# A hybrid decoder layer in float32 on one core: the activations of the weight products stored as even tokens, then odd ones, and read from the two halves in turn

## What is computed

```python
x = x + 0.5 * swiglu(rmsnorm(x), ffn1_w_gate, ffn1_w_up, ffn1_w_down)   # 2048 -> 5504 -> 2048
h = rmsnorm(x)
z = h @ w_in                                    # 2048 -> 3*1536 (q, k, v) + 1024 (u) + 2*2048 (gates)
att = dilated window attention of q, k, v in three groups of 4 heads     # 512 wide
s_out = glu(gelu(s5_ssm(u)))                                             # 1024 wide, with glu_w
merged = sigmoid(gate_a) * (att @ w_attn_branch) + sigmoid(gate_s) * (s_out @ w_ssm_branch)
x = x + merged @ w_out
x = x + 0.5 * swiglu(rmsnorm(x), ffn2_w_gate, ffn2_w_up, ffn2_w_down)
```

## Time and profile before

| | |
|---|---|
| median of 3 runs | 2240.59 us |
| span of the profiled execution | 2237.8 us |
| TensorE matmul, weight load busy | 2230.9 us, 2215.1 us |
| VectorE, ScalarE, GpSimd busy | 1347.1, 1014.1, 479.8 us |
| granted TensorE clock | 1.00 throughout |
| DMA | 528.53 MB, mean 236 GB/s |

### The profile page before, as it was taken

The page is one execution under the profiler, slowest core; times in us unless marked ns, Lnnn a source line. Parts: engine busy times, 40 slices in busy tenths (PEclk is TensorE's granted clock), DMA queues, the critical chain, the costliest instruction groups (busy, mean ns, idle before and its releaser), DMA issues.

```text
span 2237.8 us, 48675 instructions
## 1 busy us (share of the span) xinstructions
PE 2230.9 (100%) x19150; PEld 2215.1 (99%) x19150; DVE 1347.1 (60%) x1422; ACT 1014.1 (45%) x1295; POOL 479.8 (21%) x530
## 2 busy tenths in 40 slices
PE   9999999999999999999999999999999999999999
PEld 9999999999999999999999999999999999999999
DVE  7556557665455756766658867665554555545555
ACT  6554344343334545554455665444433344433443
POOL 2684313420000205664306630100000000000000
PEclk9999999999999999999999999999999999999999
DMA  7976788877776788759868875577877778777764
GB/s 239 275 236 207 241 244 273 263 236 244 244 237 206 227 262 261 218 183 317 273 193 286 260 235 188 178 230 242 260 230 229 240 242 261 227 228 241 242 202 148
DMA packets 441052, 528.53 MB, mean 236 GB/s; under 512 B 41376, under 2 KB 421712, under 8 KB 437104
## 3 DMA queue, kind: packets, MB, share of 16 engines
q1 hardware_dynamic: 425760, 508.64, 72.2%
q0 software_dynamic: 3248, 11.62, 1.5%
q10 hardware_dynamic: 11936, 6.77, 1.0%
HBM read 507.80 MB, written 106.09 MB: 274 GB/s over the span
## 4 chain that ended last, share of the span: by engine, by line
PE 99%; DMA 0%; DVE 0%; ACT 0%; SPq 0%; POOL 0%; issue 0%; POOLq 0%; ACTq 0%
PE pa L1460 32%; PE pa L1462 32%; PE pa L1461 32%; PE pb L1742 0%; DMA raw<-in_ffn_w_gate 0%; PE pb L1647 0%; PE pb L1748 0%; PE pb L1781 0%; PE pb L1707 0%; PE pb L1685 0%; PE pb L1665 0%; PE pb L1770 0%; PE pb L1581 0%; PE pb L1692 0%; PE pb L1566 0%; PE pb L1530 0%
## 5 line engine op out<-in xcount | busy, mean ns | idle before, releaser
L1015 DVE TENSOR_TENSOR w_lo<-raw,w_hi 128x1024 fp32r<-128x1024 f32 x735 | 934.9, 1282 | 620.0 <-ACT w_hi L618 615.4
L1460 PE MATMUL pa<-xg_hi,w_hi 128*128 128x264 f32 x3960 | 1131.4, 286 | 1.2 <-DVE w_lo L1015 1.2
L1461 PE MATMUL pa<-xg_lo,w_hi 128*128 128x264 f32 x3960 | 1125.2, 284 | 0.0
L1462 PE MATMUL pa<-xg_hi,w_lo 128*128 128x264 f32 x3960 | 1123.8, 284 | 0.0
L618 ACT ACTIVATE w_hi<-raw 128x1024 fp32r<-128x1024 f32 x735 | 769.1, 1056 | 754.8 <-PE pa L1462 717.0
L1460 PEld LDWEIGHTS pa<-xg_hi,w_hi 128*128 128x128 f32 x3960 | 745.3, 188 | 8.4 <-issue 6.5
L1462 PEld LDWEIGHTS pa<-xg_hi,w_lo 128*128 128x128 f32 x3960 | 744.2, 188 | 0.0
L1461 PEld LDWEIGHTS pa<-xg_lo,w_hi 128*128 128x128 f32 x3960 | 743.9, 188 | 0.2
L1461 PE MATMUL pa<-act_lo,w_hi 128*128 128x264 f32 x1632 | 463.9, 284 | 0.0
L1460 PE MATMUL pa<-act_hi,w_hi 128*128 128x264 f32 x1632 | 463.5, 284 | 0.0
L1462 PE MATMUL pa<-act_hi,w_lo 128*128 128x264 f32 x1632 | 463.1, 284 | 0.0
(11 more groups left out here) (346 smaller groups left out, 1490.2 us busy)
## 6 DMA issues: line engine op xcount, KB each, us to landing
raw<-in_ffn_w_up SPq DMA_DIRECT2D x172, 512.0 KB, 5.1
raw<-in_ffn_w_gate SPq DMA_DIRECT2D x171, 512.0 KB, 4.8
out_kv_s<-in_cache_kv_w SPq DMA_DIRECT2D x165, 512.0 KB
raw<-in_ffn_w_down SPq DMA_DIRECT2D x160, 512.0 KB, 4.5
raw<-in_w_in SPq DMA_DIRECT2D x152, 512.0 KB, 4.8
raw<-in_w_out SPq DMA_DIRECT2D x32, 512.0 KB, 4.4
tab<-ssm_tab SPq DMA_DIRECT2D x8, 1152.0 KB, 9.4
raw<-in_w_ssm_branch SPq DMA_DIRECT2D x16, 512.0 KB, 4.5
```

What stands on the lines that cost most here:

```text
L1015: dve.tensor_tensor(w_lo[:, slot], raw[:, slot], w_hi[:, slot].bitcast(f32), ALU.subtract).then_inc(lo_ready, 1)
L1460: pe.matmul(out, wh, hi, start=first, stop=False)
L1461: pe.matmul(out, wh, lo, start=False, stop=False)
L1462: return pe.matmul(out, wl, hi, start=False, stop=last)
```

## The change

Every hi and lo operand keeps its place and size, but within a tile of 264 columns the 132 even tokens stand first and the 132 odd ones behind them (halves). The splits read their source with a step of two and write the two halves (by_parity on the source). The matmuls read the operand with a pattern of two dimensions, 132 steps of one element outside and 2 steps of 132 elements inside (in_order), so that the columns enter in the order of the tokens and PSUM, its readers and all else stay as they were. For the first slab and the attention output, where prompt and sample columns are written apart, H0 and H1 name their parts of a half. No instruction is added or removed.

```diff
+    def halves(ap):
+        return ap.rearrange("p n (i j) -> p n i j", i=2)
+    def by_parity(ap):
+        return ap.rearrange("p n (j i) -> p n i j", i=2)
+    def in_order(ap):
+        return ap.rearrange("p (i j) -> p j i", i=2)
+    H0, H1 = slice(0, NT // 2), slice(NT // 2, T // 2)
...
-                    ins = act.activation(xg_hi[:, bass.ds(2 * c + u, 1), :], x_t[:, bass.ds(2 * c + u, 1), :],
+                    ins = act.activation(halves(xg_hi[:, bass.ds(2 * c + u, 1), :]), by_parity(x_t[:, bass.ds(2 * c + u, 1), :]),
                                          ACT.Copy, scale=vec[:, bass.ds(gain0 + 2 * c + u, 1)])
...
-                    ins = act.activation(xg_hi[:, k, 0:NT], pb[:, c % 4, u * NT:(u + 1) * NT], ACT.Copy, scale=vec[:, k:k + 1])
+                    ins = act.activation(in_order(xg_hi[:, k, :])[:, H0], pb[:, c % 4, u * NT:(u + 1) * NT].rearrange("p (j i) -> p j i", i=2),
+                                         ACT.Copy, scale=vec[:, k:k + 1])
...
-                                act.activation(act_hi[:, bass.ds(tile0, w), :], hid_v[:, 0:w], ACT.Copy).then_inc(acthi_ready, 1)
+                                act.activation(halves(act_hi[:, bass.ds(tile0, w), :]), by_parity(hid_v[:, 0:w]), ACT.Copy).then_inc(acthi_ready, 1)
...
-                    ins = dve.scalar_tensor_tensor(xg_lo[:, bass.ds(k, 1), :], x_t[:, bass.ds(k, 1), :],
-                                                   vec[:, bass.ds(gain0 + k, 1)], xg_hi[:, bass.ds(k, 1), :].bitcast(f32),
+                    ins = dve.scalar_tensor_tensor(halves(xg_lo[:, bass.ds(k, 1), :]), by_parity(x_t[:, bass.ds(k, 1), :]),
+                                                   vec[:, bass.ds(gain0 + k, 1)], halves(xg_hi[:, bass.ds(k, 1), :].bitcast(f32)),
                                                    ALU.mult, ALU.subtract)
...
-                                dve.tensor_tensor(act_lo[:, bass.ds(tile0, w), :], hid_v[:, 0:w],
-                                                  act_hi[:, bass.ds(tile0, w), :].bitcast(f32), ALU.subtract).then_inc(actlo_ready, 1)
+                                dve.tensor_tensor(halves(act_lo[:, bass.ds(tile0, w), :]), by_parity(hid_v[:, 0:w]),
+                                                  halves(act_hi[:, bass.ds(tile0, w), :].bitcast(f32)), ALU.subtract).then_inc(actlo_ready, 1)
...
-                pe.matmul(out, wh, hi, start=first, stop=False)
-                pe.matmul(out, wh, lo, start=False, stop=False)
-                return pe.matmul(out, wl, hi, start=False, stop=last)
+                pe.matmul(out, wh, in_order(hi), start=first, stop=False)
+                pe.matmul(out, wh, in_order(lo), start=False, stop=False)
+                return pe.matmul(out, wl, in_order(hi), start=False, stop=last)
```

More of the change, by code:

```diff
@@ L648, in sample_hi @@
                 act.wait_ge(xs_ready, 1)
-                act.activation(xg_hi[:, :, NT:T], xs_g[:], ACT.Copy).then_inc(xs_hi, 1)
+                act.activation(halves(xg_hi[:])[:, :, :, H1], by_parity(xs_g[:]), ACT.Copy).then_inc(xs_hi, 1)
             def first_split_hi(half, ready):
@@ L815, in attention @@
                     act.wait_ge(prod_ready, len(UNITS))
-                    act.activation(att_hi[:, 0:3, 0:NT], att_v[:, 0:3, 0:NT], ACT.Copy).then_inc(att_hi_ready, 1)
+                    act.activation(halves(att_hi[:, 0:3])[:, :, :, H0], by_parity(att_v[:, 0:3, 0:NT]), ACT.Copy).then_inc(att_hi_ready, 1)
                 if i == 5 and j == 0:
@@ L863, in gates_b @@
                         act.wait_ge(att_read, NSLOT)
-                        act.activation(att_hi[:, 3, 0:NT], att_v[:, 3, 0:NT], ACT.Copy).then_inc(att_hi_ready, 1)
+                        act.activation(halves(att_hi[:, 3:4])[:, :, :, H0], by_parity(att_v[:, 3:4, 0:NT]), ACT.Copy).then_inc(att_hi_ready, 1)
                     if isinstance(i, int) and i == ph.iters - 1 and j == 6:
                         act.wait_ge(pv_read, NS)
-                        act.activation(att_hi[:, :, NT:T], att_v[:, :, NT:T], ACT.Copy).then_inc(att_hi_ready, 1)
+                        act.activation(halves(att_hi[:])[:, :, :, H1], by_parity(att_v[:, :, NT:T]), ACT.Copy).then_inc(att_hi_ready, 1)
             def sigmoid(c):
@@ L953, in _ @@
                         act.wait_ge(gelu_ready, 2 * n + 2)
-                        act.activation(zs_hi[:, half], zs_v[:, half], ACT.Copy).then_inc(zhi_ready, 1)
+                        act.activation(halves(zs_hi[:, half]), by_parity(zs_v[:, half]), ACT.Copy).then_inc(zhi_ready, 1)
             def glu(i, ph=PH["glu"]):
@@ L968, in glu @@
                         act.wait_ge(evacuated, ph.group(i, g) + 1)
-                        act.activation(s_hi[:, 2 * c:2 * c + 2], up_v[:], ACT.Copy).then_inc(shi_ready, 1)
+                        act.activation(halves(s_hi[:, 2 * c:2 * c + 2]), by_parity(up_v[:]), ACT.Copy).then_inc(shi_ready, 1)
                     if i == 1 and j == 0:
@@ L979, in merged_hi @@
                 act.wait_ge(m_ready, c + 1)
-                act.activation(act_hi[:, bass.ds(2 * c, 2), :], hid_v[:], ACT.Copy).then_inc(acthi_ready, 1)
+                act.activation(halves(act_hi[:, bass.ds(2 * c, 2), :]), by_parity(hid_v[:]), ACT.Copy).then_inc(acthi_ready, 1)
             def ssm_branch(i, ph=PH["ssm_branch"]):
@@ L1031, in first_lo @@
                     k = 2 * c + u
-                    ins = dve.scalar_tensor_tensor(xg_lo[:, k, 0:NT], pb[:, c % 4, u * NT:(u + 1) * NT], vec[:, k:k + 1],
-                                                   xg_hi[:, k, 0:NT].bitcast(f32), ALU.mult, ALU.subtract)
+                    ins = dve.scalar_tensor_tensor(in_order(xg_lo[:, k, :])[:, H0], pb[:, c % 4, u * NT:(u + 1) * NT].rearrange("p (j i) -> p j i", i=2),
+                                                   vec[:, k:k + 1], in_order(xg_hi[:, k, :].bitcast(f32))[:, H0], ALU.mult, ALU.subtract)
                 ins.then_inc(xlo_ready, 1)
@@ L1047, in samples_in @@
                 dve.wait_ge(xs_hi, 1)
-                dve.tensor_tensor(xg_lo[:, :, NT:T], xs_g[:], xg_hi[:, :, NT:T].bitcast(f32), ALU.subtract)
+                dve.tensor_tensor(halves(xg_lo[:])[:, :, :, H1], by_parity(xs_g[:]), halves(xg_hi[:].bitcast(f32))[:, :, :, H1], ALU.subtract)
             def first_split_lo(half, ready, n, done):
@@ L1239, in attention @@
                     dve.wait_ge(att_hi_ready, 1)
-                    dve.tensor_tensor(att_lo[:, 0:3, 0:NT], att_v[:, 0:3, 0:NT], att_hi[:, 0:3, 0:NT].bitcast(f32),
-                                      ALU.subtract).then_inc(att_lo_ready, 1)
+                    dve.tensor_tensor(halves(att_lo[:, 0:3])[:, :, :, H0], by_parity(att_v[:, 0:3, 0:NT]),
+                                      halves(att_hi[:, 0:3].bitcast(f32))[:, :, :, H0], ALU.subtract).then_inc(att_lo_ready, 1)
             dstep = Chain(dve, dec_step)
@@ L1304, in gates_b @@
                             dve.wait_ge(att_hi_ready, 3)
-                            dve.tensor_tensor(att_lo[:, :, NT:T], att_v[:, :, NT:T], att_hi[:, :, NT:T].bitcast(f32),
-                                              ALU.subtract).then_inc(att_lo_ready, 1)
+                            dve.tensor_tensor(halves(att_lo[:])[:, :, :, H1], by_parity(att_v[:, :, NT:T]),
+                                              halves(att_hi[:].bitcast(f32))[:, :, :, H1], ALU.subtract).then_inc(att_lo_ready, 1)
                         dve.wait_ge(zi_step, 5 * k + 5)
@@ L1317, in gates_b @@
                         dve.wait_ge(att_hi_ready, 2)
-                        dve.tensor_tensor(att_lo[:, 3, 0:NT], att_v[:, 3, 0:NT], att_hi[:, 3, 0:NT].bitcast(f32),
-                                          ALU.subtract).then_inc(att_lo_ready, 1)
+                        dve.tensor_tensor(halves(att_lo[:, 3:4])[:, :, :, H0], by_parity(att_v[:, 3:4, 0:NT]),
+                                          halves(att_hi[:, 3:4].bitcast(f32))[:, :, :, H0], ALU.subtract).then_inc(att_lo_ready, 1)
                     if j % 4 == 3:
@@ L1392, in _ @@
                         dve.wait_ge(zhi_ready, g // 2 + 1)
-                        dve.tensor_tensor(zs_lo[:, half], zs_v[:, half], zs_hi[:, half].bitcast(f32), ALU.subtract).then_inc(zlo_ready, 1)
+                        dve.tensor_tensor(halves(zs_lo[:, half]), by_parity(zs_v[:, half]), halves(zs_hi[:, half].bitcast(f32)), ALU.subtract).then_inc(zlo_ready, 1)
             ph = PH["glu"]
@@ L1404, in _ @@
                         dve.wait_ge(shi_ready, c + 1)
-                        dve.tensor_tensor(s_lo[:, 2 * c:2 * c + 2], up_v[:], s_hi[:, 2 * c:2 * c + 2].bitcast(f32),
+                        dve.tensor_tensor(halves(s_lo[:, 2 * c:2 * c + 2]), by_parity(up_v[:]), halves(s_hi[:, 2 * c:2 * c + 2].bitcast(f32)),
                                           ALU.subtract).then_inc(slo_ready, 1)
@@ L1410, in merged_lo @@
                 dve.wait_ge(acthi_ready, ACT0["ssm_branch"] + c + 1)
```

(2 more changed lines are left out.)

6 lines of the change are left out of this document (3 added, 3 removed).

## The result

The changed kernel takes 2099.17 us (median of 4 runs, 2097.92 to 2100.85) against 2240.21 us: a ratio of 0.9369, 95% interval 0.9356 to 0.9383, so 6.3% faster. The forecast was 8638 us, with a range from 2232 to 8900. Rival C had 2083 us.

What follows compares the result with a forecast made beforehand. TensorE's weight products were taken as the bound: 17,568 x (485.6 - 121.45) ns adds 6397 us, splits 0, so the median of 2240.59 us becomes 8638 us; range 2232 to 8900 us.

Steps and rivals of the forecast that it cites:

- Rival C: Every weight product: neighbouring columns hit one piece mid-fetch; alternating halves give 112.5 ns each, 157 us less, 2083 us; chance 0.18.
- Bound, number, pace: TensorE's weight products set the time: 17,568 at 121.45 ns each make 2133.6 us, 95% of the span.
- The price of one product: Each weight product's stepped operand read, priced from other engines' stepped SBUF rows: 485.6 ns instead of 121.45.
- The estimate beside it: Dense stream of 264 float32 taken as 66 lines at 1.80 ns: 119 ns, near the measured pace.
- Rival A: Every weight product: TensorE no longer takes two neighbouring float32 together, 222.5 ns each, 1775 us more, 4016 us; chance 0.18.
- Rival B: Weight products: the read side holds two places at once, each half dense, so no difference, 2240.6 us; chance 0.17.
- The floor of 109 ns: Lower bound for one weight product, from the pace of nine transposes with 128-column weights; 2022 us at it.
- Splits: ScalarE and VectorE splits, read two apart, lie beside TensorE's other slabs: 0 added to the time.
- the first slab: Splits with PSUM as the source, where TensorE waits 0.4 us for xg_lo: a few tenths of a us at most.
- the worst case: Splits cost as much as with a 16-byte step and their cover goes: 60 x 0.9 us = 54 us.

Runs made afterwards that it cites:

- e2: Kernel before with only the change's storage (even tokens, then odd ones, splits read with a step of two), matmuls reading dense: 2242.57 us, ratio 1.0012.

## Why the prediction was wrong

**Bound, number, pace: right.** 17,568 products at 121.45 ns made the time, and every run of the layer here follows their pace.

**The price of one product failed, at the step called weak.** "I take 264 x 1.83 + 2.5 = 485.6 ns, because stepped SBUF reads are the nearest rows in kind". The order was to cost 364 ns a product more; it costs 8.91 ns less. Two things were wrong in it and one was not. The price of a new piece was about right: 1.76 ns on TensorE for 1.83 taken from other engines, and a reader with one stream does pay it for each column (468 ns, plain float32, step 4). Wrong was that a float32r operand has one reader: it behaves as if it had two, so that even a new piece for every element costs 224 to 260 ns and not 485.6. And wrong was what the new order looks like to each of them. I saw 0, 132, 1, 133 as a jump at every element. A stream of even columns sees 0, 1, 2, 3: fewer new pieces than before, 33 for 66.

**The estimate beside it pointed the other way.** 66 lines x 1.80 ns = 119 ns came near the measured pace, which said that the dense stream was already held by its lines. The 1.80 stands in no row (they have 1.83 to 1.88), and that 66 is the right number is luck: I counted it for one reader, and in the dense order each of two streams goes through all 66. I took this for a price only, and did not ask what an order with fewer lines per reader would gain. The rule of the Trainium skill (SBUF — State Buffer, Door 1: The DMA port swizzle, in its note on cachelines) agrees with these runs in kind, once lines are counted for each stream and not for the instruction: what crosses to new lines more often takes longer, 112.5, 118.3, 177.5 and 235 ns. The two hits on a line that it asks for as the least were not quite enough here: a stream that takes two elements of each piece needs 118.3 ns, and 130 with fours in turn, against 112.5.

**Rival A** had the right doubt, that TensorE takes two columns together, and drew from it that pulling them apart would break the pair. They need not be neighbours. **Rival B** was right that two places are held at once, and overlooked that the dense order was paying for its pieces; the time moved by 6.3%. **Rival C** had the size: 112.5 ns and 157 us less. Its mechanism, a reader that fetches for columns alternately, is nearly the one found; that neighbours hit the same piece is at most 1.7 of the 7.5 ns between dense and halves in those matmuls (118.3 to 120.0). The formula of the Trainium skill (TensorE: Matmul & The Clock Gate, Back-to-back issue gap), 264/2.4 + 2.5, which the page gives for a matmul by itself, now agrees with the trace to 0.1 ns. The floor of 109 ns isn't reached: float32r matmuls of 128 to 240 columns stay at 111.7. I gave C 0.18, for want of a row of such a reader; the 11 ns that nothing explained were the sign of one. **Its sum** was 16 us too good because it let nothing else become late; gates_b is 5.9 of them.

**Splits: nearly right.** I put 0 on the path and a few tenths of a us on the first slab; it is 2.2 us in the whole (e2), all in the start, under the 54 of the worst case. A step of 8 bytes costs ScalarE 0.10 ns an element and not 1.0, and TensorE's list shows no new wait on act_lo. For the first slab I priced a read with a step, and what costs there is another form, the halves written in turn: 0.77 to 0.89 ns an element more.

**The range** left out the faster side, on a chance of 0.18 for C that was too low.

## What to carry to other kernels

For a float32r matmul count, for even and odd columns apart, how many 16-byte pieces each goes through. Four elements in a row from each piece cost nothing extra in any run; two did, and those are what the dense order gives each stream. It shows from 240 columns on (113.3 ns for 111.7). Storing the operand so that even and odd columns are two dense runs, in any blocks of 8 or more elements, is worth 6 to 7% of a stream of 264; quarters, pairs or fours in turn or a step lose 8 to 117% against the dense order. bf16 wants the dense order. Mind who writes the operand: halves written in turn took half as long again on ScalarE, and 40% longer on VectorE, which reads the hi part in turn there as well. When a pace lies above its formula and no wait explains it, the gap may be a resource at its bound: ask which order would use less of it before pricing the new order as worse.

## What the runs showed of the hardware

A float32r moving operand behaves as two streams, one for even and one for odd columns; plain float32 behaves as one, with 222.5 ns dense, 233 at step 2, 468 at step 4 and 280 for halves in turn, for 264 columns. At steps of up to 4 a stream pays 1.76 ns for each new 16-byte piece, whatever its distance from the other stream (0 to 804 elements), and 1.7 to 2.4 ns a matmul more if both go through the same ones. At longer steps the price goes from 1.68 (step 16 of a stream) to 1.95 ns (step 40). It can return to a piece at less: quarters in turn come to (142 - 2.5) / 132 = 1.06 ns an element. Never returning is no guarantee: fours in turn come to (130 - 2.5) / 66 = 1.93 ns a piece. A dense operand that starts one element past a piece takes 125 ns, halves in turn 112.5 as before. bf16 halves in turn take 224 ns for 112.5 dense. The other two engines' prices for a step of 16 bytes or more, 1.83 and 1.88 ns, lie in the same range.
